# The first modulation in two halves of columns, two projections in two turns, and a position bias that a transfer turns

## The reference

```python
c_act = jax.nn.silu(c)
mod = c_act @ w_ada[l] + b_ada[l]                       # 1024 x 3072
shift, scale, gate = jnp.split(mod, 3, axis=-1)
h = rmsnorm(x, norm_g[l]) * (1.0 + scale[:, None]) + shift[:, None]
proj = h @ w_in[l]                                      # 13 parts: qm, km, vm, om, zm, im, fm, qa, ...
qk = jax.nn.silu(causal_dwconv(jnp.concatenate([qm, km], axis=-1), conv_w[l], conv_b[l]))
...
bias = table[t5_bucket(jnp.maximum(rel, 0))]            # rel = query - key, one value for each head
bias = jnp.where((rel >= 0)[..., None], bias, -jnp.inf).transpose(2, 0, 1)
p = jax.nn.softmax(logits + bias[None, :, None], axis=-1)
```

## Time and profile before

| | |
|---|---|
| median of three runs | 1648.84 us |
| the profiled execution | 1648.3 us |
| its span, first to last instruction | 1646.3 us |
| TensorE busy | 1264.4 us (77% of the span) |
| weight loads of TensorE busy | 684.2 us (42%) |
| VectorE busy | 571.3 us (35%) |
| ACT busy | 426.0 us (26%) |
| POOL busy | 35.8 us (2%) |
| HBM | 334 GB/s over the span, 549.41 MB read |
| mean granted TensorE clock | 0.884 of full |

### The profile page before, as it was taken

How to read it: one execution, slowest core, us unless ns; L and a number is a source line. 1 busy time by engine, 2 the same in 40 slices (tenths; PEclk the granted TensorE clock), 3 DMA queues, 4 the chain that set the end, 5 groups by cost and what they waited for, 6 DMA issues and landing times.

```text
span 1646.3 us, 18014 instructions
## 1 busy us (share of the span) xinstructions
PE 1264.4 (77%) x7278; PEld 684.2 (42%) x7278; DVE 571.3 (35%) x955; ACT 426.0 (26%) x644; POOL 35.8 (2%) x60
## 2 busy tenths in 40 slices
PE   3999999999999989877656665756665666665764
PEld 1877877777787779731111111111111111111111
DVE  2676446667657784731101101110110110111012
ACT  1657336677545664420000000000000000000000
POOL 1000000001000000000000000000000000000000
PEclk8999999999999999978888778787888878788687
DMA  9565547676666553789999999999999999999995
GB/s 352 193 242 210 191 162 267 229 269 242 248 240 216 184 174 125 292 348 429 429 427 428 428 427 429 428 428 427 429 426 429 427 428 429 427 429 427 428 427 236
DMA packets 87425, 551.66 MB, mean 335 GB/s; under 512 B 6104, under 2 KB 6424, under 8 KB 58672
## 3 DMA queue, kind: packets, MB, share of 16 engines
q1 hardware_dynamic: 84256, 541.09, 80.7%
q0 software_dynamic: 2800, 9.14, 1.7%
q10 hardware_dynamic: 288, 0.30, 0.1%
HBM read 549.41 MB, written 1.09 MB: 334 GB/s over the span
## 4 chain that ended last, share of the span: by engine, by line
PE 51%; DMA 34%; DVE 9%; ACT 3%; issue 2%; SPq 0%; POOL 0%; DVEq 0%; POOLq 0%; ACTq 0%
PE ps L531 48%; DMA b<-in_w_down 32%; DVE b L1286 4%; PE ps L535 3%; ACT b L952 2%; DMA b<-in_w_ada 2%; DVE b L1926 1%; DVE b L1894 1%; DVE b L1896 1%; DVE b L1303 1%; POOL b L1961 0%; DVE b L1296 0%; SPq L457 0%; DVE b L1317 0%; DVE b L1902 0%
## 5 line engine op out<-in xcount | busy, mean ns | idle before, releaser
L531 PE MATMUL ps<-b,b 128*32 128x512 f32 (+3 forms) x6922 | 1204.7, 554 | 303.8 <-DMA b<-in_w_up 105.7
L531 PEld LDWEIGHTS ps<-b,b 128*32 128x32 f32 (+2 forms) x6922 | 637.2, 157 | 824.3 <-issue 294.6
L1286 DVE TENSOR_TENSOR b<-b,b 128x1024 fp32r<-128x1024 f32 (+6 forms) x261 | 283.8, 1088 | 213.0 <-ACT b L952 198.3
L952 ACT ACTIVATE b<-ps 128x512 f32<-128x512 f32 (+3 forms) x180 | 98.2, 545 | 891.9 <-PE ps L531 581.0
L952 ACT ACTIVATE b<-b 128x1024 fp32r<-128x1024 f32 (+4 forms) x223 | 221.7, 994 | 268.7 <-PE ps L531 153.0
L1916 DVE TENSOR_TENSOR b<-b,ps 128x512 f32<-128x512 f32 x16 | 11.0, 688 | 402.4 <-issue 385.8
L1926 DVE TENSOR_TENSOR b<-b,ps 128x1024 f32<-128x1024 f32 x28 | 34.2, 1221 | 332.1 <-PE ps L531 332.1
L535 PE MATMUL ps<-b,b 128*128 128x128 f32 x356 | 71.3, 333 | 66.8 <-DVE b L1317 26.9
L535 PEld LDWEIGHTS ps<-b,b 128*128 128x128 f32 x356 | 47.9, 173 | 125.7 <-DVE b L1317 37.7
L1286 DVE TENSOR_TENSOR b<-ps,b 128x512 f32<-128x512 f32 (+7 forms) x63 | 34.5, 548 | 11.7 <-ACT b L954 4.7
L1961 POOL TENSOR_TENSOR b<-b,b 128x1 f32<-128x1 f32 (+3 forms) x15 | 13.1, 873 | 1117.6 <-DVE b L1296 1117.6
(11 more groups left out here) (51 smaller groups left out, 158.5 us busy)
## 6 DMA issues: line engine op xcount, KB each, us to landing
b<-in_w_gate SPq DMA_DIRECT2D x64, 2048.0 KB, 40.7
b<-in_w_up SPq DMA_DIRECT2D x64, 2048.0 KB, 40.7
b<-in_w_down SPq DMA_DIRECT2D x63, 2048.0 KB, 34.2
b<-in_w_in SPq DMA_DIRECT2D x74, 1024.0 KB, 6.3
b<-in_w_ada SPq DMA_DIRECT2D x36, 1024.0 KB, 8.3
b<-in_w_proj_m SPq DMA_DIRECT2D x8, 1024.0 KB, 7.4
b<-in_w_out SPq DMA_DIRECT2D x8, 1024.0 KB, 4.9
b<-in_w_proj_a SPq DMA_DIRECT2D x4, 1024.0 KB, 5.0
```

Source lines behind the costliest of these rows:

```text
L531: return e.matmul(o, lhsT, rhs, start=start, stop=stop, skip_group_check=True)
L952: e.activation(o, i, f, bias=bias, scale=scale).then_inc(mark[0], 1)
L1286: e.tensor_tensor(o, a, b, op).then_inc(mark[0], 1)
```

## The change

It has three parts. First, w_ada's columns come in two halves: half i holds columns 512 i to 512 i + 511 of the shift and of the scale, so k-tiles 0 to 3 of the tokens for i = 0 and 4 to 7 for i = 1. Each half is eight transfers of 512 KB. TensorE's uses of banks 7 and 6 double (`R00`, `R01`, `R0F0`, `R0F1`), with 256 columns in each of the four groups. Behind the first half TensorE goes over to the projections and does the second half's k-tiles 0 to 3 after half-step (0, 0), 4 to 6 after (0, 1) and 7 with the turning after (0, 2). VectorE and ACT do the second half's modulation at (0, 1).

Second, the order of the slots is V0, Q0, V1, K0, V2, Q1, V3, K1, and the first two are interleaved: V0 and Q0 on the first four k-tiles, then V0 and Q0 on the others. What hung on slots 1 to 7 (convolutions, copies of V, gates) moves by one slot; the bias row moves to (1, 2), its mask to (3, 1).

Third, the bias row goes to a scratch of 2 MB, 128 times for each head, by four transfers out of the eight partitions; `BIAS` is read from it with a step of 511 between partitions, which gives the turned rows directly. The mirror matrix, `BREV`, the four matmuls and ACT's copies are gone.

```diff
-    ("Q0", "T", "w_in", QM, "H"), ("V0", "N", "w_in", VM, "H"), ("K0", "T", "w_in", KM, "H"), ("V1", "N", "w_in", VM + W, "H"),
+    ("V0", "N", "w_in", VM, "H"), ("Q0", "T", "w_in", QM, "H"), ("V1", "N", "w_in", VM + W, "H"), ("K0", "T", "w_in", KM, "H"),
...
-        if name in ("WO0", "WP0"):
+        if name in ("V0", "WO0", "WP0"):
             other = SLOTS[s + 1][0]
-            order = (0, 1, 2, 3) if name == "WO0" else (2, 3, 0, 1)
+            order = (2, 3, 0, 1) if name == "WP0" else (0, 1, 2, 3)
...
-            def ada0(k):
-                e.dma_start(ADA0[k], dram["w_ada"][k * P:(k + 1) * P, 0:2048]).then_inc(S(f"ada0_{k}"), 16)
+            def ada0(i, k):
+                for s in range(2):
+                    c0 = s * D + i * W
+                    src = dram["w_ada"][k * P:(k + 2) * P, c0:c0 + W].rearrange("(k p) n -> p k n", p=P)
+                    e.dma_start(ADA0[:, i, k:k + 2, s * W:(s + 1) * W], src).then_inc(S(f"ada0_{i}_{k}"), 16)
...
-            for k in range(7):
-                ada0(k)
+            for k in range(0, KD, 2):
+                ada0(0, k)
             ring_load(0)
-            ada0(7)
-            for i in range(1, len(LOADS)):
+            for k in range(0, KD, 2):
+                ada0(1, k)
+                if k == 2:
+                    ring_load(1)
+            for i in range(2, len(LOADS)):
                 ring_load(i)
...
+            def ada0(i, k):
+                if k == 0:
+                    begin(f"R0{i}")
+                e.wait_ge(S(f"ada0_{i}_{k - k % 2}"), 32)
+                for n in range(4):
+                    ins = mm(ps[32 * n:32 * n + 32, 7, 0:T], crep[:, k, :], ADA0[:, i, k, n * T:(n + 1) * T],
+                             k == 0, k == KD - 1)
+                if k == KD - 1:
+                    ins.then_inc(FULL[7], 1)
+                    begin(f"R0F{i}")
+                    e.wait_ge(*free(f"R0{i}"))
+                    for b in range(2):
+                        ins = flip(ps[:, 6, b * P:(b + 1) * P], MOD0[i][:, b * P:(b + 1) * P])
+                    ins.then_inc(FULL[6], 1)
...
             for g, ts in UNITS:
                 half(g, ts)
...
+                if s == 0 and c < 3:
+                    for k in ((0, 1, 2, 3), (4, 5, 6), (7,))[c]:
+                        ada0(1, k)
...
-                if (s, c) == (7, 0):
-                    bias_turn(0)
-                    bias_turn(1)
-                if (s, c) == (7, 2):
-                    bias_turn(2)
-                    bias_turn(3)
...
+                if (s, c) == (0, 1):
+                    e.wait_ge(*free("R0F1"))
+                    e.wait_ge(S("v_mod"), 1)
+                    for q in (2, 3):
+                        modulate_hi(f"XT{q}", HTH, GS, SH)
...
+            def modulation(i):
+                e.wait_ge(*full(f"R0{i}"))
+                copy(MOD0[i], ps[:, 7, 0:T], to=free(f"R0{i}"))
+                e.wait_ge(*full(f"R0F{i}"))
...
+                modulate(f"XT{2 * i + 1}", GS, SH)
+                modulate_lo(f"XT{2 * i}", 1, HTL, HTH)
+                modulate_lo(f"XT{2 * i + 1}", 1, HTL, HTH)
+
+            modulation(0)
             lo(2)
...
                 lo(g + AHEAD)
+                if (s, c) == (0, 1):
+                    modulation(1)
...
-                if s in (1, 3, 5, 7) and c < 3:
-                    conv(*{1: ("Q0", QT, 0), 3: ("K0", KT, 8), 5: ("Q1", QT, 4), 7: ("K1", KT, 12)}[s], c)
+                if s in (2, 4, 6, 8) and c < 3:
+                    conv(*{2: ("Q0", QT, 0), 4: ("K0", KT, 8), 6: ("Q1", QT, 4), 8: ("K1", KT, 12)}[s], c)
...
-            load(toep.rearrange("(h j) -> h j", h=AH), brow, "toep_in")
-            e.wait_ge(S("toep_in"), 16)
-            load(BREV, bass.AP(toep.tensor, 0, [[1, P], [2 * T, AH], [1, T]]), "brev_in")
+            for i in range(4):
+                load(toep.rearrange("(h i r j) -> h i r j", h=AH, i=4, r=P // 4)[:, i], brow.unsqueeze(1).broadcast_to([AH, P // 4, 2 * T]), "toep_in")
+            e.wait_ge(S("toep_in"), 64)
+            load(BIAS, bass.AP(toep.tensor, P - 1, [[2 * T - 1, P], [P * 2 * T, AH], [1, T]]), "bias_turned")
```

More of the change, by code:

```diff
@@ L50 @@
 _lay(CONST, ("ident", P), ("iota", P), ("causal", P))
-_lay(EARLY, ("selh", MH * P), ("onehot", 2 * T), ("future", 2 * T), ("mirror", P))
+_lay(EARLY, ("selh", MH * P), ("onehot", 2 * T), ("future", 2 * T))
 _lay(LATE, ("before", NT * T), ("ahead", NT * T), ("behind", NT * T), ("n1", T), ("n2", T),
@@ L79, in constants @@
     put(early, EARLY, "future", np.broadcast_to(np.where(dist >= 0, 0.0, NEG), (AH, 2 * T)).astype(np.float32))
-    put(early, EARLY, "mirror", (p + j == P - 1).astype(np.float32))
     late = np.zeros((P, LATE["all"][1]), np.float32)
@@ L141, in _halves @@
                     add(which, order[a + j], a + j == 0, a + j == 3, (s + i // 2, 2 * (i % 2) + j))
-        elif name not in ("WO1", "WP1"):
+        elif name not in ("Q0", "WO1", "WP1"):
             for kp in range(n):
@@ L190, in _bank_uses @@
         uses[b].append(name + "b")
[L191 to L194, removed]
+    misc = {4: [], 5: [], 6: [], 7: ["R00", "R01", "R1", "R2", "R3", "R4"]}
+    misc[6] += ["R0F0", "R0F1", "GATE", "GF"]
+    misc[4] += ["NM0"]
+    misc[5] += ["BROW", "NM1"]
     for h in range(MH):
@@ L352, in build @@
         w2, b2 = part(cols, COLS, "conv_w_2").rearrange("p (j c) -> p j c", j=3), part(cols, COLS, "conv_b_2")
-        ADA0 = [at(8 * k, 2048) for k in range(KD)]
-        MOD0 = at(82, W)
+        ADA0 = at(0, 2 * KD, 2 * W).rearrange("p (i k) n -> p i k n", i=2)
+        MOD0 = [at(82 + i, T) for i in range(2)]
         XN, XJ = at(66, NT, D), at(74, NT, D)
@@ L365, in build @@
         QAT, KAT, VAN, BIAS = at(50, AH, T), at(58, AH, T), at(66, NT, D), at(74, AH, T)
-        BREV, HA = at(82, AH, T), at(82, NT, D)
+        HA = at(82, NT, D)
         early = at(90, EARLY["all"][1])
@@ L620, in gate_rows @@
                 ins.then_inc(FULL[b], 1)
[L622 to L626, removed]
             def mlstm_scores(h):
@@ L726, in _ @@
                 flip_pair(f"XT{q}", XN, 2 * q)
-            begin("R0")
+            def ada0(i, k):
[12 more added lines that the diff above has]
+                    ins.then_inc(FULL[6], 1)
             e.wait_ge(S("v_crep"), 1)
             for k in range(KD):
[L730 to L738, removed]
+                ada0(0, k)
             for g, ts in UNITS:
@@ L1046, in _ @@
                 hi(g)
[L1047 to L1050, removed]
+            e.wait_ge(*free("R0F0"))
+            for q in range(2):
                 modulate_hi(f"XT{q}", HTH, GS, SH)
@@ L1064, in _ @@
                         conv_silu(name, dst, c0)
-                if s in (2, 4, 6, 8) and c == 0:
-                    n = s // 2 - 1
+                if (s, c) in ((1, 2), (3, 0), (5, 0), (7, 0)):
+                    n = s // 2
                     rows(f"V{n}", lambda t: HM[:, t, n * W:(n + 1) * W])
-                if (s, c) == (2, 1):
+                if (s, c) == (3, 1):
                     e.wait_ge(S("v_gabs"), 1)
                     act(gt1, gt1, ACT.Exp, scale=-1.0, to=S("a_gabs"))
-                if (s, c) == (5, 0):
+                if (s, c) == (6, 0):
                     e.wait_ge(S("v_gm"), 1)
                     act(gf, gf, ACT.Exp, scale=-1.0, to=S("a_gf"))
-                if (s, c) in ((6, 3), (7, 0)):
-                    for h in (0, 1) if s == 6 else (2, 3):
+                if (s, c) in ((7, 3), (8, 0)):
+                    for h in (0, 1) if s == 7 else (2, 3):
                         e.wait_ge(*free(f"NM{h // 2}"))
@@ L1078, in _ @@
                         act(ET[:, h, 2 * P:3 * P], ET[:, h, 2 * P:3 * P], ACT.Exp, bias=ccol[:, 1, h:h + 1], to=S("a_et"))
[L1079 to L1082, removed]
                 if s in (9, 11) and c == 0:
@@ L1436, in _ @@
                 lo(g)
[L1437 to L1450, removed]
+            def modulation(i):
+                e.wait_ge(*full(f"R0{i}"))
+                copy(MOD0[i], ps[:, 7, 0:T], to=free(f"R0{i}"))
+                e.wait_ge(*full(f"R0F{i}"))
+                v = ps[:, 6, 0:T].rearrange("p (b n j) -> p n b j", b=2, n=4)
+                gs, sh, bsc, bsh = (a[:, 4 * i:4 * i + 4].rearrange("p (n b) -> p n b", n=2) for a in (
+                    GS, SH, part(cols, COLS, "b_sc"), part(cols, COLS, "b_sh")))
+                tt(gs, v[:, 2:4, :, 0], bsc, ALU.add)
+                stt(GS[:, 4 * i:4 * i + 4], GS[:, 4 * i:4 * i + 4], 1.0, part(cols, COLS, "norm_g")[:, 4 * i:4 * i + 4], ALU.add, ALU.mult)
+                tt(sh, v[:, 0:2, :, 0], bsh, ALU.add, to=free(f"R0F{i}"))
+                modulate(f"XT{2 * i + 1}", GS, SH)
+                modulate_lo(f"XT{2 * i}", 1, HTL, HTH)
+                modulate_lo(f"XT{2 * i + 1}", 1, HTL, HTH)
+            modulation(0)
             lo(2)
@@ L1492, in attn_logits @@
                 if h == 0:
-                    for j in (2, 3):
-                        e.wait_ge(*free(f"BT{j}"))
```

(15 more changed lines are left out.)

22 lines of the change are left out of this document (11 added, 11 removed).

## The result

The changed kernel takes 1677.34 us (median; 1676.96 to 1678.77) against 1649.03 (1648.56 to 1650.37) of the kernel before on the same chip: 1.0172 times as long, 95% interval 1.0159 to 1.0185. The forecast was 1653.3 with a range of 1637 to 1669: right in the sign, and the time lies outside. The profiled execution takes 1676.96 us, 1675.2 of them its span, so 28.9 more than the span before, with the clock granted at 0.874 (0.884).

A forecast was written before the change was run, and what follows sets the result against it. The prediction took TensorE to bound the kernel for some 500 us after a late start. Its terms, - 3.0 - 3.4 - 5.6 + 14.8 + 1.7 = + 4.5, gave 1652.8, or 1653.3 us beside the median; range 1637 to 1669.

The forecast's parts named there:

- Head, -3.0: Kernel start: modulation in halves lets TensorE's projections begin earlier, worth 3.0 us (bounds -1 to 4).
- Bias turns, -3.4: TensorE-bound stage: four mirror matmuls go, each two passes 0.43 us apart, saving 3.4 us.
- Old gap, -5.6: TensorE's gap at 97.76 us goes: 3.9 us, plus 1.7 lost to the half clock, 5.6 in all.
- load late by 4.0, gap of 3.9: Weight load beside the 1 MB scratch read landed 4.0 us late; no slack, so TensorE's gap was 3.9 us.
- K1's convolution in slot 8, 0 (at worst 2): 6.0 us of VectorE moved into 158.92 to 175.5 us, busy 7.6 of 16.6: fits, cost 0, at worst 2 us.
- The scratch's packets: 2 MB bias write: slow packets on eight engines delay the weight load 14.8 us; 1649 to 1659, chance 0.32.
- with 0.46 us for 4 KB and, as in the 16 KB write, one engine for each head: 2 MB write: 4 KB packets take 0.46 us, one engine per head, 64 such packets on every engine.
- Eleven are through when the weight load starts; each of the load's 32 packets per engine then waits for one: Weight load beside the write, end of slot 3: 32 x 0.46 = 14.8 us late, TensorE with it.
- Source-paced on sixteen engines: Rival for the write: 4 KB packets take 0.93 us on all sixteen engines; 1662.9 us, chance 0.24 (1659 to 1670).
- 24.4 + 1.7: Rival's cost: 26 packets of 0.93 us stand before the weight load, 24.4 us late, plus 1.7 for the clock.
- The estimate from the Trainium skill's port rule: Write from two ports of about 27 GB/s each: 2 MB take 38.5 us, sixteen-engine case about 1668.5; no own chance.
- Full speed: Rival: the write's 4 KB packets take 0.165 us; 1636.8 on sixteen engines, 1643.5 on eight, taken as 1640; chance 0.28.

The follow-up runs named there:

- undisturbed old order: Kernel before, its slot order and one modulation kept, with 256 KB bias write from 128 partitions near slot 8, read back in next load pause: 1644.12 us.
- candidate: Changed kernel with 16 copies per head (256 KB) written from 128 partitions near 165 us, read back by eight transfers near 182: 1640.76 us, ratio 0.995.
- one-port source: Changed kernel with the same 2 MB written from partitions 0 to 3 and 32 to 35 instead of 0 to 7: 1717.54 us in one run.

## Why the prediction was wrong

- **Head, -3.0: near, and its exact fit partly luck.** In the changed kernel's trace the landmarks come within 1.3 us and slot 3's end within 0.3. But that trace is the earliest of the nine with the new order (slot 3 ends at 94.5 to 96.8, the middle one at 95.5), and the trace before is the latest of the three with the old one (97.1 to 97.8). Between the middle ones the head is worth 2.0 us.
- **Bias turns, -3.4: fits**, though no run isolates it. The undisturbed old order is 4.1 us early at the shared chain piece (450.25): 3.4, and 0.7 of gaps.
- **Old gap, -5.6: too large.** The step "load late by 4.0, gap of 3.9" took the whole gap for the load's. With no transfer beside it the same place still costs 1.55 us and two later ones 0.87 and 0.77; the conversion, the subtraction and the convolution behind the load are late by themselves. In the undisturbed old order a slow clock in 130 to 160 us (granted 0.94, 1.8 us) comes on top, so only some 0.6 of the 5.6 was to be had there, going by this one profile. In the changed kernel this is hidden by the larger gap.
- **K1's convolution in slot 8, 0 (at worst 2): nearly right.** The candidate's gap of 0.77 at 160.65 waits for a step of VectorE that stands behind this convolution's, which in turn stood behind the load of 6.07 us.
- **The scratch's packets: the step that failed.** The forecast was "with 0.46 us for 4 KB and, as in the 16 KB write, one engine for each head"; it measured 1.17 us, on sixteen engines. Two things went into it. The rate: 69 GB/s (8 x 2 KB in 0.23 us is rather 71), from the last packet of a 16 KB write; a long write from these partitions gets 50 to 53. The engines: one transfer does keep eight (48%), as I took it, but four at once keep sixteen, each engine with half the rate. The second alone leaves the bytes per second where they are, and takes the free half from the weight loads. The Trainium skill says of POOL's transfers that those of fewer engines move round the sixteen (DMA: Bandwidth & Descriptors, "Why a DMA increments its semaphore by 16 and not by 1"); 48% for one and 95% for four agree.
- **"Eleven are through when the weight load starts; each of the load's 32 packets per engine then waits for one": half right.** The turns are one for one (129 to 122), but only late: 9 packets of the load in 112 to 120 us. Until 117 the load moved nothing, and then the write was so near its end that it became the load's. The kernel with one transfer shows this step by itself, on the eight engines that the forecast had assumed: 32.0 us late, where turns at its 0.61 us for a packet make 19.5. 14.8 us late was forecast, 36.9 measured (41.9 from issue to ACT, less 5.0).
- **The rivals.** Source-paced on sixteen engines was the case; at 24.4 + 1.7 it too was short, since it used the same 69 GB/s. The estimate from the Trainium skill's port rule came nearer, with a write of 38.5 us; POOL waited 42.7. Its time was mis-summed: by the rule that gave 24.4 (what is left of the write when the load should start), 38.5 - 5.3 = 33.2 us late make 1671.7, not 1668.5. I had given the row of a lone packet more weight than a rule of the Trainium skill that spoke to exactly this source. "Full speed" is what the 128-partition source does: 1641.6, in place of the 1640 taken for it.

With the measured packets and the forecast's own other terms: -3.0 - 3.4 - 5.6 + 36.9 + 1.7 = + 26.6, of the 28.3 measured.

## What to carry to other kernels

Count the source partitions of a large transfer by the ports that they reach, not by how many they are, nor by groups of four neighbours alone: for the same 2 MB POOL waited 6.4 us with all 128 partitions, 42.7 with 0 to 7, and 89.5 with 0 to 3 and 32 to 35. A slow transfer costs its neighbours first; before you save matmuls with a DMA, ask which loads are issued while it runs, and spread its source or put it into their pauses (here the two came out alike, 1641.6 and 1640.8 us, the second with an eighth of the bytes). And a gap that ends with a late load isn't all the load's: look what its consumer would do with the load on time.

## What the hardware showed that I had not expected

- A load of SP's queue, issued 3 us after POOL's write began, had moved nothing 17 us later (no row of its queue in 95 to 112) with all engines at 95%; with the one-port source it had no row in 94 to 147 either. Meanwhile SP's issue of a single load took 8.09 and 17.38 us.
- Four transfers of 512 KB in a row keep sixteen engines where one of 2 MB keeps eight, at the same total rate: the gap was 32.0 us instead of 36.8 (1674.8 us in one run, beside 1677.3).
- The granted clock falls to half for some 3 us also where TensorE was busy ahead of it (near 153 in the kernel with the first two parts alone, 1.7 us; near 135 in the old order with the late bias; not in the candidate's profile). What brings it about wasn't found.
